# A two-layer decoder trunk on one core: large expert items read gate and up in whole rows, all column chunks at once

## The reference

```python
def swiglu(u, w_gate, w_up, w_down):
    return (jax.nn.silu(u @ w_gate) * (u @ w_up)) @ w_down

    logits = (tok @ router).astype(jnp.float32)
    top_v, top_i = lax.top_k(logits, TOP_K_EXPERTS)      # 2 of 8
    ...
    for e in range(N_EXPERTS):
        out = out + gates[:, e:e + 1].astype(tok.dtype) * swiglu(tok, w_gate[e], w_up[e], w_down[e])
```

## Time and profile before

| | us |
|---|---|
| median of 3 runs (1268.98 to 1270.40) | 1270.13 |
| the profiled execution | 1269.83 |
| its span, first to last instruction | 1268.1 |
| PE busy in the span | 1234.1 (97%) |
| DVE busy | 637.3 (50%) |
| ACT busy | 565.2 (45%) |
| DMA | 424.48 MB, mean 335 GB/s |

### The profile page before, as it was taken

How to read it: one execution, slowest core, us unless ns; L and a number is a source line. 1 busy time by engine, 2 the same in 40 slices (tenths; PEclk the granted TensorE clock), 3 DMA queues, 4 the chain that set the end, 5 groups by cost and what they waited for, 6 DMA issues and landing times.

```text
span 1268.1 us, 18552 instructions
## 1 busy us (share of the span) xinstructions
PE 1234.1 (97%) x7266; PEld 875.2 (69%) x7266; DVE 637.3 (50%) x755; ACT 565.2 (45%) x871; POOL 99.5 (8%) x260
## 2 busy tenths in 40 slices
PE   9998999999999999999999999999999999999787
PEld 8988999999989944588853468884347887332232
DVE  6887765555765501488831168880226886010001
ACT  6665554443655511477730167770036775010001
POOL 1000000000000183100002100000310000110000
PEclk9999999999999999999999999999998999999999
DMA  9943544348533399999999999999999999999997
GB/s 329 373 139 129 199 173 173 122 166 264 194 117 117 134 425 428 403 412 416 428 423 426 421 407 415 416 426 423 428 407 412 415 424 384 423 429 423 426 429 293
DMA packets 89032, 424.48 MB, mean 335 GB/s; under 512 B 5457, under 2 KB 24050, under 8 KB 71282
## 3 DMA queue, kind: packets, MB, share of 16 engines
q1 hardware_dynamic: 88592, 422.76, 83.4%
q10 hardware_dynamic: 354, 0.54, 0.1%
HBM read 422.23 MB, written 1.05 MB: 334 GB/s over the span
## 4 chain that ended last, share of the span: by engine, by line
PE 87%; DMA 8%; DVE 2%; ACT 1%; SPq 1%; issue 1%; ACTq 0%; POOLq 0%; POOL 0%; DVEq 0%
PE psA L2067 9%; PE psY L2082 7%; PE psA L1694 7%; PE psB L2067 7%; PE psA L1696 7%; PE psA L1695 7%; PE psB L1694 7%; PE psB L1696 7%; PE psB L1695 7%; PE psY L1696 5%; PE psY L1695 5%; PE psY L1694 5%; DMA ring<-in_moe_w_gate 3%; DMA ring<-in_moe_w_up 2%; DMA ring<-in_moe_w_down 2%; PE psY L2035 1%
## 5 line engine op out<-in xcount | busy, mean ns | idle before, releaser
L1560 DVE TENSOR_TENSOR wlo<-ring,whi 128x2048 fp32r<-128x2048 f32 (+1 forms) x138 | 287.7, 2104 | 88.3 <-ACT whi L938 86.0
L938 ACT CAST whi<-ring 128x1024 fp32r<-128x1024 f32 x252 | 260.4, 1052 | 100.8 <-issue 34.6
L1307 DVE TENSOR_TENSOR wlo<-ring,whi 128x1024 fp32r<-128x1024 f32 (+2 forms) x104 | 152.3, 1484 | 19.4 <-ACT whi L754 19.3
L2067 PE MATMUL psA<-ring,resT 128*64 128x512 f32 x620 | 148.8, 597 | 13.2 <-DMA ring<-in_moe_w_gate 6.7
L754 ACT CAST whi<-ring 128x1024 fp32r<-128x1024 f32 (+1 forms) x134 | 133.4, 1023 | 60.4 <-PE psY L1696 28.2
L1625 DVE TENSOR_TENSOR rowbuf<-psY,rowbuf 128x512 f32<-128x512 f32 x28 | 18.6, 688 | 211.9 <-PE psY L2035 211.9
L2067 PE MATMUL psB<-ring,resT 128*64 128x512 f32 (+1 forms) x624 | 113.9, 486 | 0.0
L1694 PE MATMUL psA<-xhi,whi 128*128 128x256 f32 x368 | 105.0, 285 | 2.6 <-DVE wlo L1307 1.2
L1694 PE MATMUL psB<-xhi,whi 128*128 128x256 f32 x368 | 106.4, 289 | 0.0
L2067 PEld LDWEIGHTS psB<-ring,resT 128*64 128x64 f32 x624 | 44.9, 137 | 89.0 <-issue 89.0
L1695 PE MATMUL psA<-xlo,whi 128*128 128x256 f32 x368 | 102.8, 279 | 0.0
(11 more groups left out here) (364 smaller groups left out, 2148.3 us busy)
## 6 DMA issues: line engine op xcount, KB each, us to landing
ring<-in_moe_w_down SPq DMA_DIRECT2D x50, 2048.0 KB, 19.9
ring<-in_moe_w_gate SPq DMA_DIRECT2D x35, 1792.0 KB, 10.8
ring<-in_moe_w_up SPq DMA_DIRECT2D x32, 1792.0 KB, 17.7
ring<-in_moe_w_gate SPq DMA_DIRECT2D x18, 2048.0 KB, 20.1
ring<-in_moe_w_up SPq DMA_DIRECT2D x18, 2048.0 KB, 21.4
ring<-in_ffn_w_gate SPq DMA_DIRECT2D x5, 2048.0 KB, 7.8
ring<-in_ffn_w_up SPq DMA_DIRECT2D x5, 2048.0 KB, 8.0
ring<-in_ffn_w_down SPq DMA_DIRECT2D x5, 2048.0 KB, 7.9
```

What stands on the lines that cost most here:

```text
L938: nc.scalar.copy(hi_of(NG + m, 2), item_part(ring, j, g, 2)).then_inc(hi_done, 2)
L1307: nc.vector.tensor_tensor(part_of(wlo, s, g, size), part_of(ring, s, g, size), f(hi_of(m, size)), ALU.subtract).then_inc(lo_done, size)
L1560: nc.vector.tensor_tensor(item_part(wlo, j, g, step), item_part(ring, j, g, step), f(hi_of(NG + m, step)), ALU.subtract).then_inc(lo_done, ...
L2067: ins = mm(few_bank(b)[half * FEW:(half + 1) * FEW, to:to + end - x], few_in[:, k, :], raw[:, x - q * W:end - q * W], start=k == 0, stop=k ...
```

## The change

A large item now has the order of a small one. Its slots are eight row blocks of gate (seven cells, rows of 14 KB), eight of up, then seven slots of down. Gate keeps all seven chunks in seven PSUM banks at once; ACT takes the seven silus out of them, up fills the same banks, and the result goes to psA. A row block is one transfer, or two where the ring's end cuts it. The first two slots, which came in four transfers of 512 KB each, come in three of 2, 2, 3 and of 3, 2, 2 cells. Splitting and halving go by pieces of up to 2 and 4 cells that end at a slot's end, at a ring slot's end and at the end of `whi`: 92 pieces for ACT instead of 84, 57 for DVE. In a small item the four banks change places, and the third waits for the copy of the last item's result.

```diff
-    IS = len(item_slots)
+    IS = 3 * NE
...
+    item_slots = [(kind, k) for kind in ("gate", "up") for k in range(KD)] + [("down", d) for d in range(NE)]
...
+    HI_PIECES, LO_PIECES = split_pieces(2, 2), split_pieces(2, 4)
+    LO_AT = dict(LO_PIECES)
+    FIRST_PARTS = [[2, 2, 3], [3, 2, 2]]
...
         def few_bank(b):
-            return (psA if b < 2 else psB)[:, b % 2, 0:BANKS[b]]
+            return (psB[:, 0, :], psB[:, 1, :], psA[:, 1, :], psA[:, 0, :])[b][:, 0:BANKS[b]]
+
+        def big_bank(c):
+            return (psA[:, 0, :], psA[:, 1, :], psB[:, 0, :], psB[:, 1, :], psY[:, 1, :], psY[:, 2, :], psY[:, 0, :])[c]
...
             def big_item(i, e):
...
+                for j, (kind, at) in enumerate(item_slots):
+                    sp.reg_add(used_past, used_past, item_cells[j])
+                    sp.wait_ge(group_used, used_past)
                     if kind == "down":
...
+                    w = moe_w_gate if kind == "gate" else moe_w_up
+                    src = w[0][e, at * P:(at + 1) * P, :]
                     if j < 2:
...
+                        for a, n in enumerate(FIRST_PARTS[j]):
+                            sp.dma_start(to[:, q * W:(q + n) * W], src[:, q * W:(q + n) * W]).then_inc(
+                                first_full[j][a] if a < len(FIRST_PARTS[j]) - 1 else item_full[j], 16)
+                            q += n
+                        continue
+                    for to, q, n in few_runs(i, j):
+                        sp.dma_start(to, src[:, q * W:(q + n) * W]).then_inc(item_full[j], 16)
...
             def expert(i):                                     (ACT)
...
+                for k in range(KD - 1):
+                    done = item_split(i, done, item_from[k + 1] + AHEAD + 2)
+                for c in range(NE):
+                    act.wait_ge(group_used, used_at(i, item_from[KD - 1] + c + 1))
+                    nc.scalar.activation(in_blocks(big_act(c)), by_block(big_bank(c)), ACT.Silu).then_inc(m_silu, 1)
+                    done = item_split(i, done, item_from[KD - 1] + c + 1 + AHEAD + 2)
+                for k in range(KD - 1):
+                    done = item_split(i, done, item_from[KD + k + 1] + AHEAD + 2)
+                done = item_split(i, done, 2 * CELLS + 4)
+                hidden_hi(i, 0)
+                done = item_split(i, done, 2 * CELLS + GS)
+                hidden_hi(i, 1)
+                for d in range(NE):
+                    done = item_split(i, done, 2 * CELLS + GS * (d + 1) + AHEAD + 2)
+                    if d + 2 < NE:
+                        hidden_hi(i, d + 2)
...
             def expert(i):                                     (DVE)
...
+                for j in range(2 * KD - 1):
+                    done = item_halve(i, done, item_from[j + 1] + AHEAD)
+                multiply(i, 0)
+                multiply(i, 1)
+                done = item_halve(i, done, 2 * CELLS + 4)
+                hidden_lo(i, 0)
+                hidden_lo(i, 1)
+                done = item_halve(i, done, 2 * CELLS + GS)
+                multiply(i, 2)
+                done = item_halve(i, done, 2 * CELLS + GS + 4)
+                multiply(i, 3)
+                for d in range(NE):
+                    if d + 2 < NE:
+                        hidden_lo(i, d + 2)
+                    done = item_halve(i, done, 2 * CELLS + GS * (d + 1) + AHEAD)
+                    if d + 4 < NE:
+                        multiply(i, d + 4)
...
+            def big_columns(i, j, kind, k):                    (PE)
...
+                for c in range(NE):
+                    m = item_from[j] + c
+                    if m in LO_AT:
+                        pe.wait_ge(lo_done, split_at(i, m + LO_AT[m]))
...
+                    if kind == "up" and k == 0:
+                        pe.wait_ge(m_silu, i * NE + (c + 1))
+                    three(big_bank(c), ihi[:, k, :], ilo[:, k, :], whi_of(NG + m), item_part(wlo, m, 1)[:, 0, :],
+                          k == 0, k == KD - 1).then_inc(group_used, 1)
+                    if kind == "up" and k == KD - 1 and 3 <= c < 5:
+                        hidden_turn(i, c - 3)
+
+            def big_down(i, j, c):
+                pe.wait_ge(m_hlo, hlo_at(i, max(c, 1)))
                 for g in range(GS):
...
+                    if m in LO_AT:
+                        pe.wait_ge(lo_done, split_at(i, m + LO_AT[m]))
...
             def expert(i):
...
+                    big_down(i, j, at)
+                    if at + 2 < NE:
+                        hidden_turn(i, at + 2)
```

More of the change, by code:

```diff
@@ L164, in trunk @@
[L164 to L170, removed]
+    END_GATHER = [item_slot["down", 1], item_slot["down", 2]]
@@ L171, in trunk, with split_pieces @@
+    NEXT_SMALL_AT = item_slot["down", 6]
+    SUM_AT = {item_slot["up", 7]: (0, 1), item_slot["down", 3]: (1, 1), item_slot["down", 4]: (0, 0), item_slot["down", 5]: (1, 0)}
+    BIG_GATHER = item_from[item_slot["down", NE - 2]]
+    SPREAD_AT = item_slot["up", 6]
+    SCATTER_AT = [item_slot[at] for at in (("gate", 7), ("up", 1), ("up", 5), ("up", 6))]
     CELLS = GS * RING
     AHEAD_CELLS = GS * AHEAD_SLOTS
+    BIG_FROM = GS * ((NS + SHIFT) % RING)
+    def split_pieces(first_size, size):
+        pieces, m = [], 0
+        for j in range(FS):
+            end = item_from[j] + item_cells[j]
+            while m < end:
+                n = min(first_size if j < 2 else size, end - m, HL - (NG + m) % HL, GS - (BIG_FROM + m) % GS)
+                pieces.append((m, n))
+                m += n
+        return pieces
@@ L527, in transfers @@
         def transfers(i, j):
-            kind, at = few_slots[j]
+            kind, at = item_slots[j]
+            if not few(i):
+                return len(few_runs(i, j)) if j >= 2 else 1
             if kind != "down":
@@ L928, in _, with item_split @@
             nc.scalar.copy(count[:, 1, :], before[:, :]).then_inc(count_set, 1)
[L930 to L938, removed]
+            def item_split(i, done, last):
+                while done < len(HI_PIECES) and HI_PIECES[done][0] < last:
+                    m, size = HI_PIECES[done]
+                    j = max(a for a in range(FS) if item_from[a] <= m)
+                    if j < 2 and first_part(j, m + size - 1) < len(FIRST_PARTS[j]) - 1:
+                        for a in range(first_part(j, m), first_part(j, m + size - 1) + 1):
+                            act.wait_ge(first_full[j][a], 16 * (BIG_AT.index(i) + 1))
+                    else:
+                        act.wait_ge(item_full[j], landed_at(i, j))
+                    act.wait_ge(group_used, hi_free(i, m, size))
+                    nc.scalar.copy(hi_of(NG + m, size), item_part(ring, m, size)).then_inc(hi_done, size)
+                    done += 1
+                return done
             def gather_hi(i, q):
@@ L1006, in result @@
                 for half, part in enumerate(parts):
-                    nc.scalar.copy(part, psY[:, 0 if few(i) else half, :]).then_inc(y_out, 2 // len(parts))
+                    nc.scalar.copy(part, psY[:, 0, :] if few(i) else psA[:, half, :]).then_inc(y_out, 2 // len(parts))
             def few_rows(i):
@@ L1035, in expert @@
             def expert(i):
[L1036 to L1046, removed]
-                            nc.scalar.activation(in_blocks(hid_of(d)), by_block(psA[:, half_of(d), :]), ACT.Silu).then_inc(m_silu, 1)
+                done = sum(1 for m, size in HI_PIECES if m < NE)
+                for k in range(KD - 1):
[14 more added lines that the diff above has]
+                        hidden_hi(i, d + 2)
                 for q in range(2):
@@ L2056, in few_columns @@
                         pe.wait_ge(rs_set, 1)
+                    if kind == "gate" and k == 0 and b == 2 and isinstance(i, int) and i:
+                        pe.wait_ge(y_out, 2 * i)
                     todo = []
```

209 lines of the change are left out of this document (82 added, 127 removed).

## The result

The changed kernel takes 1344.26 us (median of 6 runs, 1342.29 to 1345.83) against 1269.06 us of the kernel before, measured beside it: a ratio of 1.059, 95% interval 1.0577 to 1.0604. It is slower by 75 us. The forecast was 1348 in a range of 1317 to 1360, with a chance of 0.92 for slower.

A forecast was written before the change was run, and what follows sets the result against it. PE's pace was taken as the bound up to item 6, transfers behind it. From 1269.8 us, old waits took off 8.15, new waits added 59.1 (1320.8) and clock falls 27.5, giving 1348, range 1317 to 1360.

The forecast's parts named there:

- DVE's order in the down slots: DVE waits for chunk d + 2 before halving slot d + 1, delaying PE: 17.2 us per large item.
- The half wait at d = 0: First down slot: half the next slot is halved beforehand, giving PE 2.8 us of work; 1.2 us delay.
- Gate to up: Turn where ACT has seven silus and splits of about seven cells: 0.3 us per large item, between 0 and 2.
- up to down: Turn where PE waits to transpose chunk 0, then chunk 1: together 2.2 us per large item, between 0 and 4.
- The old waits: PE's two waits for the late third slot, in items 3 and 5, go, with one clock fall: -8.15 us.
- The clock: PE's granted clock falls to 1.2 GHz after ten of twelve new waits: 27.5 us, bounds 0 and 33.
- The sum without the clock: 1269.8 - 8.15 + 59.1 = 1320.8 us: old waits gone, new waits in three large items, no clock falls.
- After item 5: Transfers are again at the ring's limit when PE ends item 5, so the remaining 194 us stay.
- rival (d): Cut transfers each hold the queue a fixed time; six with 2 us delay the third slot: 1287 us, chance 0.01.
- Rows of 14 KB at nothing: Longer rows gain a large item about 3 us of transfer time, costed at nothing while PE is the bound.
- held by the ring anyhow: At a large item's end the transfers have filled the ring and wait for PE, so faster rows gain nothing.
- Three transfers for the first slots: Cutting the first two slots costs nothing, as 512 KB transfers landed 1.34 us apart, nearly the stream's rate.

The follow-up runs named there:

- e1: The changed kernel, but in the down loop DVE halves to the end of slot d + 1 before it waits for chunk d + 2; 1272.26 us.
- e2: The kernel before, with only DVE's order turned round: it waits for the transposed chunks before it halves the next slot; 1366.68 us.
- e7: e4, but the halvings of four cells at 64 and at 116 are each cut into two of two; 1262.88 us.
- e4: e1, but DVE multiplies chunks 0 and 1 before halving cells 112 to 115, and ACT rounds chunk 1 before splitting 116 to 119; 1267.45 us.
- e8: The changed kernel, with sixteen unused identity products on PE behind the transposes of down slots 1 to 4, inside each long wait; 1322.10 us.
- e6: e4, but each of a large item's first two slots comes in one transfer instead of three; 1267.65 us.
- e5: e4, but a large item's gate and up come in transfers of two cells, rows of 4 KB, first two slots too; 1269.64 us.
- e9: e7, but a large item's gate and up come in transfers of two cells, rows of 4 KB; 1268.73 us.

## Why the prediction was right, point by point

- **DVE's order in the down slots**: right, and shown from both sides by e1 and e2. Forecast four delays of 4.0 us with about 3.8 idle per large item; measured idle 3.64 to 3.69. The half wait at d = 0 was put at a delay of 1.2; it idled 0.80.
- **Gate to up, and up to down**: forecast 0.3, 0.85 and 1.35; measured 0.29, 0.72 and 1.25.
- **The old waits**: forecast to go, 8.15 us. In the changed kernel, and in e1 and e7, no wait for the third slot is left; in e4 one of 0.27 us is, so that the lead at item 5 is thin. e7, which has no other wait up to item 6 either, is 5.5 us under the kernel before in the medians. In the spans it is 7.5 (1260.6 against 1268.1), but the profiled execution of before, from which the 8.15 us were read, was 1.4 us longer than the median beside e7.
- **The clock**: 27.5 forecast and 22.2 measured by e8. That this is near is in part luck, two errors of opposite sign. I let ten of the twelve waits slow the clock; all twelve did. I priced each at the 2.75 us of the one case in the earlier trace rows; from the starts of the products, less 0.2335 us each, they cost 1.4 to 2.5, 1.83 in the mean. The term that was mis-sized is the price of one fall.
- **The sum without the clock**: 1320.8 forecast, 1322.1 measured. Against three times item 1 of before, which has no wait, the large items are 82 us longer (148.8 us in the mean instead of 121.3); less 22 of clock that is 60 us of waits, where the sum had 59.1. The 4 us by which 1348 was over the measured 1344.3 are this 1.3 short and the clock's 5.3 too much.
- **After item 5**: 194 us forecast, 194.4 found.
- **Two slips in the working**: the upper bounds of both turns add 3 x (1.7 + 1.8) = 10.5 us to the range, not 6, so its end should have been 1364. In rival (d) the third slot would be ready at 4.3 + 2.3 + 12 = 18.6 us, not 18.3. Neither bears on the forecast.
- **Rows of 14 KB at nothing**: right in the changed kernel, whose loads idle in every down slot. But the step "held by the ring anyhow" fails where PE is fast: with rows of 4 KB the loads no longer stand at the ring's limit at the end of item 5, and whole rows give 5.8 us, some 3 of them behind it. What share is the rows' and what the larger transfers', no run separates.
- **Three transfers for the first slots**: nothing in the time, as forecast, by e6. The page "DMA: Bandwidth & Descriptors" of the Trainium skill (section "Anatomy of one DMA") gives about 2.0 us fixed for a transfer on GpSimd's path, and puts it down to completion for the most part. It does not say that queued transfers pay it one after another, as rival (d) had it, and on SP's queue they did not: 512 KB each 1.34 us.

## What to carry to other kernels

When a loop over stages is rewritten, compare for each engine what it still does before each wait, not only what it does in a stage: here DVE had all its work and lost its lead of one slot, because a wait moved ahead of it by two lines. Price such a wait by the whole loop of engines (transpose, round, subtract, halve: 4.0 us here) and add the clock. An engine that idles half its time can still be the bound. And once a bound is mended, test the parts that were worth nothing again: the longer rows, put at nothing beside the waits of the 1344 us kernel, gave 5.8 us at 1263.

## What the runs showed of the hardware

- PE's wait of 3.04 us (before) and the twelve of 3.64 to 3.69 us in the changed kernel were all followed by the clock's lower level, 0.50 granted, that is 1.2 GHz; the wait of 2.04 us in the kernel before and those of 1.25 and 0.80 us in the changed one were not. In e2 one wait of 3.69 us was not either, and behind five others of 3.60 to 3.69 us PE ran at the upper level for another 0.6 to 1.3 us first, so the length of a wait alone does not settle it. Behind the twelve nearly equal waits of the changed kernel the clock came back after 3.0 to 5.6 us, so that the price of one ranged from 1.4 to 2.5 us.
- Sixteen small products within each wait kept the clock at 1.00 and won 22.2 us while the waits themselves stayed: adding work to PE made the changed kernel faster.
- In windows of 20 us at the start of the large items, transfers of two cells with rows of 4 KB (e5, e9) ran at 405 to 406 GB/s, and whole row blocks with rows of 14 KB (e6, e7) at 424 to 427, both with the DMA engines at a busy share of 1.01 to 1.03. The two slots cut in three, rows of 4 and 6 KB, came at 412 to 424 (e4), whole at 427 to 433 (e6), in the 9 us in which they land; in the time that made no difference.
